# Moving a recurrence's last stage and the latent preparations into the operators' stage

## The reference, cut to what matters

```
rwkv7 (6 heads):  state = state * w_t - (state . kk_t) b_t + v_t k_t ;  y_t = state . r_t
gated delta (6):  A = tril(k k^T * decay * beta, -1);  u, w = solve(I + A, [v*beta, k*beta*exp(gc)])
                  per chunk: delta = u - w S;  o = q S + attn delta;  S = d S + k^T delta
latent attention: q = rms(c_q) w_uq;  kv = rms(c_kv) w_ukv;  ang = positions * inv_freq
                  rope with cos(ang), sin(ang) on 32 of 96 columns; softmax; times v
out:              gates silu(gate), group norms, w_out, then the feed-forward layer
```

## Time and profile before

| | us |
|---|---|
| median of 3 runs | 2176.77 |
| fastest run | 2175.23 |
| profiled execution, its own time | 2175.9 |
| its span | 2174.1 |

### The profile page before, as it was taken

One profiled execution on the slowest core, in us unless ns is written; L12 is line 12 of the kernel. 1 busy time (PEld: TensorE's weight loads), 2 busy tenths in 40 slices (PEclk: granted clock), 3 DMA queues, 4 the chain that ended last, 5 costly groups with the idle time before them and its releaser, 6 DMA issues. The chain is left out here.

```text
span 2174.1 us, 35768 instructions
## 1 busy us (share of the span) xinstructions
PE 2119.3 (97%) x14084; PEld 1693.3 (78%) x14084; DVE 1294.8 (60%) x1761; ACT 908.6 (42%) x1422; POOL 119.5 (5%) x96
## 2 busy tenths in 40 slices
PE   9999999999999999999999999999887899999999
PEld 6888788888877777778888887777777467888887
DVE  7565676663379877576665349596465566433333
ACT  5444532222366666652222236555332545323221
POOL 0000011110000000001111000000243000000000
PEclk9999999999999999999999999999999899999999
DMA  7331333333324221323333332222000112333331
GB/s 270 101 133 39 88 116 96 96 96 97 96 73 150 80 71 48 106 71 109 97 96 102 97 97 78 85 84 81 3 4 4 47 39 70 114 96 98 97 96 67
DMA packets 54231, 189.77 MB, mean 87 GB/s; under 512 B 5984, under 2 KB 6240, under 8 KB 53984
## 3 DMA queue, kind: packets, MB, share of 16 engines
q1 hardware_dynamic: 53824, 187.49, 28.1%
q10 hardware_dynamic: 288, 0.59, 0.1%
HBM read 184.91 MB, written 3.15 MB: 86 GB/s over the span
## 5 line engine op out<-in xcount | busy, mean ns | idle before, releaser
L303 PE MATMUL l_banks<-l_r_hi,l_w_hi 128*128 128x512 f32 x1440 | 573.5, 398 | 2.5 <-DVE l_r_lo L1544 2.3
L305 PE MATMUL l_banks<-l_r_hi,l_w_lo 128*128 128x512 f32 x1440 | 561.0, 390 | 0.0
L304 PE MATMUL l_banks<-l_r_lo,l_w_hi 128*128 128x512 f32 x1440 | 560.8, 389 | 0.0
L282 ACT ACTIVATE l_w_hi<-ring 128x1024 fp32r<-128x1024 f32 x217 | 228.4, 1056 | 280.6 <-PE l_banks L305 278.0
L288 DVE TENSOR_TENSOR l_w_lo<-ring,l_w_hi 128x1024 fp32r<-128x1024 f32 x217 | 299.8, 1384 | 73.4 <-ACT l_w_hi L282 69.8
L303 PEld LDWEIGHTS l_banks<-l_r_hi,l_w_hi 128*128 128x128 f32 x1440 | 270.3, 188 | 71.2 <-issue 8.2
L304 PEld LDWEIGHTS l_banks<-l_r_lo,l_w_hi 128*128 128x128 f32 x1440 | 270.5, 188 | 57.1 <-issue 3.8
L305 PEld LDWEIGHTS l_banks<-l_r_hi,l_w_lo 128*128 128x128 f32 x1440 | 270.3, 188 | 57.3
L303 PE MATMUL mt_a<-net_r_hi,net_w_hi 128*128 128x512 f32 x352 | 137.3, 390 | 0.0
L305 PE MATMUL mt_a<-net_r_hi,net_w_lo 128*128 128x512 f32 x352 | 137.0, 389 | 0.0
L304 PE MATMUL mt_a<-net_r_lo,net_w_hi 128*128 128x512 f32 x352 | 136.9, 389 | 0.0
(11 more groups left out here) (566 smaller groups left out, 3542.7 us busy)
## 6 DMA issues: line engine op xcount, KB each, us to landing
ring<-weights SPq DMA_DIRECT2D x314, 512.0 KB, 3.6
na_bias<-window_bias SPq DMA_DIRECT2D x16, 512.0 KB, 5.5
da_rel<-t_rel SPq DMA_DIRECT2D x8, 448.0 KB, 4.6
outT<-X SPq DMA_DIRECT2D x12, 256.0 KB, 2.1
X<-xT SPq DMA_DIRECT2D x8, 256.0 KB, 5.2
const<-consts SPq DMA_DIRECT2D x1, 1312.0 KB, 10.4
l_pt<-pT SPq DMA_DIRECT2D x2, 512.0 KB, 9.7
X<-outT SPq DMA_DIRECT2D x4, 256.0 KB, 3.2
```

The costliest lines, as they stand in the source:

```text
L282: act.activation(self.w_hi[:, c % self.slots, :], k.ring[:, g % RING, :], ACT.Copy).then_inc(self.w_rounded, 1)
L303: pe.matmul(psum, hi, self.hi(rhs_slot), start=start, stop=False)
L304: pe.matmul(psum, hi, self.lo(rhs_slot), start=False, stop=False)
L305: return pe.matmul(psum, lo, self.hi(rhs_slot), start=False, stop=stop)
```

## The change

1. The stage `recurrence` is gone. Its carries and outputs of pair 5 (`carry_last`, `outputs_last`) stand at the end of the operators' stage. Its preparations stand within pair 5: the four transfers on SP after earlier conditions, ScalarE's work in pieces after levels 2, 3 and 4 of pair 5, VectorE's angles before `carry_out(1)` and their reduction after `carry_out(6)`, TensorE's sums after `finish_yn`.
2. A second buffer M, `m2`: masks alternate, and a mask waits for the level before the last one.
3. `chunk_ends(1)` and `(2)` move from behind `mask(i, 0)` to behind `mask(i, 2)`.
4. `setup_akr(0)` stands before `turn_u(0)`, `invert_x(0, 0)` rather than behind them.
5. States of the recurrence live in other tiles, and the eight banks of PSUM (`hy_ps`) are held over both stages.

```diff
@@ -2168,22 +2168,23 @@
         v_tok = st.sb("v_tok", [P, 2, TT, P])
         b_tok = st.sb("b_tok", [P, TT, P])
         ki_tok = st.sb("ki_tok", [P, TT, P])
-        more = st.sb("more", [P, 2, W])
+        m2 = st.sb("m2", [P, U8, CHUNK])
...
-        ps = st.ps("ps", [P, 8, S])
         P_B = 2
         SETUP = (3, 4, 7)
         F0, F1 = 5, 6
...
-        homes = [unused[:, j * W:(j + 1) * W] for j in range(3)] + [more[:, 0, :], more[:, 1, :], b_tok[:, :, :].rearrange("p t s -> p (t s)")[:, 0:W]]
+        unused = [akr[:, 0, :, :, :].rearrange("p u k l -> p (u k l)"), kx[:, 0, :, :].rearrange("p u l -> p (u l)")]
+        homes = [unused[j // 3][:, j % 3 * W:(j % 3 + 1) * W] for j in range(5)] + [b_tok[:, :, :].rearrange("p t s -> p (t s)")[:, 0:W]]
         def state(c):
@@ -2191,6 +2192,16 @@
                 return n0[:, 0:EARLY, 0, :]
             return homes[c - 2].rearrange("p (n d) -> p n d", d=CHUNK)
+        squares = [k.H[:, j, :] for j in (0, 2, 4)]
+        last_homes = ki_tok[:, :, :].rearrange("p t s -> p (t s)").rearrange("p (c d) -> p c d", d=CHUNK)
+        r32 = slice(0, MLA_ROPE)
+
+        def last_state(c):
+            return n0[:, PAIRS - 1, 0, :] if c == 1 else last_homes[:, c - 2, :]
+
+        def last_bank(c):
+            return F1 if c % 2 else SETUP[2]
+
         def y_bank(c):
             return S_B if c == NCH - 1 else SETUP[1 + (c + 1) % 2]
@@ -2256,6 +2267,17 @@
             return slice(t * P + c * CHUNK, t * P + c * CHUNK + CHUNK)
         with k.nc.Block() as block:
+            @block.sync
+            def _(sp):
+                sp.wait_ge(s["q_out"], MIX_T + 1)
+                sp.dma_start(la.pos, bass.AP(k.dram["positions"].tensor, 0, [[0, P], [1, S]])).then_inc(s["pos_loaded"], 16)
+                sp.wait_ge(s["a_ps"], PAIRS)
+                sp.wait_ge(s["ar_ps"], PAIRS)
+                sp.dma_start(la.mc, k.dram["mla_consts"]).then_inc(s["mc_loaded"], 16)
+                sp.dma_start(la.uq, k.dram["w_uq"]).then_inc(s["up_loaded"], 16)
+                sp.dma_start(la.ukv, k.dram["w_ukv"]).then_inc(s["up_loaded"], 16)
+                sp.wait_ge(s["up_loaded"], 32)
+
             @block.tensor
             def _(pe):
@@ -2443,7 +2465,7 @@
                         for pair in DIAG:
                             for c, h in pair:
                                 u = TT * h + t
-                                mm = pe.matmul(xt_ps(h, t)[half(c ^ h)], M[half(c), u, :], U[i % 2][half(c), u, :], start=True, stop=True)
+                                mm = pe.matmul(xt_ps(h, t)[half(c ^ h)], M[n % 2][half(c), u, :], U[i % 2][half(c), u, :], start=True, stop=True)
                     mm.then_inc(s["xt_ps"], 1)
@@ -2501,18 +2523,34 @@
                                            keys(n)[half(h), c * CHUNK:(c + 1) * CHUNK], start=True, stop=True)
                     mm.then_inc(s["y_ps"], 1)
+                def carry_last(c):
+                    if c >= 2:
+                        pe.wait_ge(s["carried"], NCH - 2 + c - 1)
+                    for h in range(2):
+                        mm = pe.matmul(ps[half(h), F0, 0:CHUNK], mt[half(h), last, c, :], last_state(c)[half(h), :], start=True, stop=True)
+                    mm.then_inc(s["carry_ps"], 1)
+
+                def outputs_last(c):
+                    if c == NCH - 1:
+                        pe.wait_ge(s["carried"], NCH - 2 + c - 1)
+                    pe.wait_ge(s["y_added"], 2 * (NCH - 1) + max(c - 2, 0))
+                    for h in range(2):
+                        mm = pe.matmul(ps[half(h), last_bank(c), 0:CHUNK], last_state(c)[half(h), :],
+                                       keys(last)[half(h), c * CHUNK:(c + 1) * CHUNK], start=True, stop=True)
+                    mm.then_inc(s["y_ps"], 1)
+
                 last = PAIRS - 1
                 setup_a(0)
                 setup_ar(0)
                 setup_tokens(0)
                 for i in range(PAIRS):
                     nxt = i + 1 < PAIRS
+                    if i == 0:
+                        setup_akr(0)
                     turn_u(i)
                     invert_x(i, 0)
                     if i:
                         finish_wu(i - 1)
-                    else:
-                        setup_akr(0)
                     invert_p(i, 0)
                     if i:
@@ -2563,6 +2601,22 @@
                 outputs(6)
                 outputs(7)
                 finish_yn(last)
+                pe.wait_ge(s["lat_squared"], 3)
+                pe.wait_ge(s["u_out"], LV * PAIRS)
+                pe.matmul(la.ms[:, 0, :], k.c("ones"), squares[0], start=True, stop=False)
+                pe.matmul(la.ms[:, 0, :], k.c("ones"), squares[1], start=False, stop=True).then_inc(s["lat_summed"], 1)
+                pe.wait_ge(s["yn_out"], 2 * PAIRS)
+                pe.wait_ge(s["mt_out"], PAIRS)
+                carry_last(1)
+                for c in range(1, NCH):
+                    outputs_last(c)
+                    if c == 1:
+                        pe.matmul(la.ms[:, 1, :], k.c("ones"), squares[2], start=True, stop=True).then_inc(s["lat_summed"], 1)
+                    elif 2 <= c < 2 + TT:
+                        at = (c - 2) * P
+                        pe.matmul(la.ms[:, 2, c - 2:c - 1], squares[2][:, at:at + P], k.c("ones")[:, 0:1], start=True, stop=True).then_inc(s["lat_summed"], 1)
+                    if c + 1 < NCH - 1:
+                        carry_last(c + 1)
             @block.scalar
@@ -2643,14 +2697,38 @@
                     if nxt:
                         tokens(i + 1)
                     xt_out(i, 2)
+                    if not nxt:
+                        act.wait_ge(s["masked"], LV * EARLY)
+                        act.wait_ge(s["wu_ps"], EARLY)
+                        for j in range(3):
+                            act.activation(squares[j], la.cg[j], ACT.Square).then_inc(s["lat_squared"], 1)
                     xt_out(i, 3)
+                    if not nxt:
+                        act.wait_ge(s["lat_squared"], 3)
+                        for j in range(3):
+                            act.activation(la.cg[j], la.cg[j], ACT.Copy, scale=k.p("q_norm", j) if j < 2 else k.p("kv_norm")).then_inc(s["lat_scaled"], 1)
+                        act.wait_ge(s["mc_loaded"], 16)
+                        act.wait_ge(s["gq_done"], 1)
+                        act.activation(la.c("rot4"), la.c("rot4"), ACT.Copy, scale=la.gq[:, 1:2]).then_inc(s["lat_scaled"], 1)
+                        act.activation(la.c("rot_rep", r32), la.c("rot_rep", r32), ACT.Copy, scale=k.p("k_qk", 1, r32)).then_inc(s["lat_scaled"], 1)
                     xt_out(i, 4)
+                    if not nxt:
+                        for j in range(MIX_T):
+                            act.activation(pi[:, G_GATE + j, :], pi[:, G_GATE + j, :], ACT.Silu).then_inc(s["silued"], 1)
                     if nxt and not delta(i + 1):
                         x1(i + 1)
                     if not delta(i):
                         keys_out(i)
                 wu_out(PAIRS - 1)
+                act.wait_ge(s["trig"], 1)
+                act.activation(la.sn, la.r, ACT.Sin).then_inc(s["sin_done"], 1)
+                act.activation(la.cs, la.r, ACT.Sin, scale=0.5).then_inc(s["sin_done"], 1)
+                act.preload_act_table_set(LN_EXP)
                 yn_out(PAIRS - 1)
+                act.wait_ge(s["silued"], MIX_T)
+                act.wait_ge(s["lat_scaled"], 5)
+                act.wait_ge(s["sin_done"], 2)
+                act.wait_ge(s["lat_summed"], 2 + TT)
             @block.gpsimd
@@ -2678,11 +2756,11 @@
                 def mask(i, lv):
                     n = LV * i + lv
-                    if n:
-                        pool.wait_ge(s["xt_ps"], n)
+                    if n >= 2:
+                        pool.wait_ge(s["xt_ps"], n - 1)
                     if lv == 0:
                         pool.wait_ge(s["a_out"], 2 * i + 2)
-                    pool.tensor_tensor(M, A[i % 2], over(level(lv + 1)), ALU.mult).then_inc(s["masked"], 1)
+                    pool.tensor_tensor(M[n % 2], A[i % 2], over(level(lv + 1)), ALU.mult).then_inc(s["masked"], 1)
                 mask(0, 0)
                 chunk_ends(0)
@@ -2691,6 +2769,8 @@
                     nxt = i + 1 < PAIRS
                     mask(i, 1)
                     mask(i, 2)
+                    if 0 < i < MIX_T:
+                        chunk_ends(i)
                     if nxt and delta(i + 1):
                         decay_masks(i + 1)
                     mask(i, 3)
@@ -2699,8 +2779,6 @@
                         diagonal(i)
                     if nxt:
                         mask(i + 1, 0)
-                        if not delta(i + 1):
-                            chunk_ends(i + 1)
             @block.vector
@@ -2841,6 +2919,30 @@
                         dve.tensor_tensor(out, out, ps[:, y_bank(c), at:at + to * CHUNK].rearrange("p (n d) -> p n d", d=CHUNK),
```

(44 more changed lines are left out.)

119 lines of the change are left out of this document (8 added, 111 removed).

## The result

The changed kernel takes 2164.76 us (median of five, 2158.93 to 2166.09), against 2176.77 of the kernel before beside it (three runs, 2175.23 to 2177.77): ratio 0.9946, interval 0.9935 to 0.9957, or 11.8 us less. A second set, on a chip where the kernel before took 2174.19, gave 0.9952 (0.9938 to 0.9965), 10.4 us less by the ratio and 9.5 by the two medians. Two further runs of the kernel before, of 3394.2 and 3028.5 us, are left out of all comparisons. The forecast was 2167.5 us, 8.85 less than the profiled execution before. The range held and the class (within 2%) was right; by the ratios the forecast gain was 1.5 to 3 us too small.

The account below looks back on a forecast made before the run. TensorE, busy 97% of the span, sets most of the time; the recurrence stage is a chain no engine fills. -7.25 - 1.5 - 0.7 + 0.6 = -8.85 from 2175.9 gives 2167.05, 2167.9 against the median; said 2167.5, range 2162 to 2173.

Parts of the forecast that it names:

- The end of the recurrence, -7.25: From pair 5's n0 to the mixer's end: 1.1 for sums, 6.0 carries and outputs, 1.0 stage change; 8.1 replaces 15.35 us.
- The rival with the sums at the low clock: Sums over partitions ahead of the carries at low clock: 2.55 us less gain, 2170; 25%, alone or with angles held.
- The first pair, -1.5: Pair 0: key products in TensorE's idle time and a mask wait of 0.79 gone save about 1.5 us (0.7 to 2.0).
- The scalings, -0.7: Preparation of pair 1: moved scalings no longer hold L2795 (1.53 to 0.68 us); 0.7 us less, nothing taken for pair 2.
- The angles, +0.6: Pair 5, VectorE's angles ahead of carry_out(1), partly held by POOL's masks: 0.6 us lost on the path, between 0 and 2.3.
- Its upper end of 2.3: Angles in pair 5 held by POOL's mask and `diagonal`: 2.3 us lost rather than 0.6, giving 2169.
- ScalarE's pieces and the reduction: Pair 5 preparations on ScalarE, and VectorE's reduction of 2.5 us before add_outputs(4): nothing lost, at most 0.5 us each.
- The slow rival: TensorE's instruction blocks late beside the transfers: one delay 2171, three 2178.5; one or two 4%, three or more 3%.
- that one wrong sign (over 1 us): TensorE rows with "issue" of over 1 us behind the transfers would show the prediction wrong.
- a better clock in the mixer's end: At the mixer's end's start ScalarE and VectorE split weights whatever TensorE's clock; a better clock gives a microsecond at most.

Follow-up runs that it names:

- one_buffer: The changed kernel with one masked-A buffer in place of two, each mask waiting for the product before it; 2164.43 us, ratio 0.9953 to the kernel before.
- transfers_ahead: The kernel before with only the recurrence stage's four transfers issued in the operators' stage, where the changed kernel issues them; 2171.37 us, ratio 0.9989 to the kernel before.
- merge_alone: The changed kernel with second buffer, early key products and moved scalings undone; the recurrence stays merged into the operators' stage; 2166.55 us, ratio 0.9962 to the kernel before.
- after_again: The changed kernel run once more, unchanged, on another chip; 2164.73 us, ratio 0.9952 to the kernel before.
- warm_end: The changed kernel plus six TensorE products without use behind outputs_last(2) to outputs_last(7); 2163.95 us, ratio 0.9949 to the kernel before.
- keys_behind: The changed kernel with pair 0's key products behind invert_x(0, 0) again; 2166.68 us, ratio 0.9964 to the kernel before.
- spread_warm: The changed kernel with the third sum cut into four products behind outputs_last(2) to (5), plus two products without use; 2162.41 us, ratio 0.9947 to the kernel before.

## Why the prediction came out as it did

- **The end of the recurrence, -7.25.** Right in mechanism and nearly in size: -7.83, the same to 0.01 in every merged kernel that leaves the end alone. Within it the sums came out at 0.76 behind n0 rather than 1.10, the carries and outputs at 5.39 behind the sums rather than 6.0, the stage change at 1.37 rather than 1.00. In the 5.39 the period was 0.69 rather than 0.65, and the third sum added 0.75 rather than 1.13. The rival with the sums at the low clock did not occur.
- **The first pair, -1.5.** The step that was mis-sized. It measured 2.5 at pair 0's second copy and 2.0 by pair 3. Each part went the way that was said, and further: from the stage's start, update 0 begins 2.0 us earlier (10.02 to 8.00) for 1.2 forecast, and level 1's `invert_x` 2.7 (12.19 to 9.51) for 1.5. The sum took the key products as they were, 1.78 us for 27, and did not ask why: they ran at the low clock, after the very pause into which the change moves them. The whole 32 take 1.10 at the full clock. Also its credit was wrong: the mask wait goes by the order of the products, and the second buffer does nothing (one_buffer).
- **The scalings, -0.7.** Failed. The row became short in after as said and TensorE's wait of 0.72 went, but the row was long by where POOL's instructions fell in one execution: with the scalings where they were it is 1.77 (beside a mask, transfers_ahead) and 0.69 (merge_alone), with them moved 0.68 (after) and 1.77 (after_again). The step took one trace's meeting of two instructions for a property of the order.
- **The angles, +0.6.** The lock was judged rightly by the two-input rows and the skill's rule: the Trainium skill (SBUF — State Buffer, section "Who interferes with whom") lets `tensor_scalar` contend, and the rows of 1.40 and 1.15 against 0.43 agree. Its upper end of 2.3 did not follow, since VectorE was idle there and TensorE's gap of 0.87 "issue" is at 1678.83 still. The path lost 0.1 in the mean of nine traces, and 0.6 to 0.7 in the two of the changed kernel.
- **The rest.** ScalarE's pieces and the reduction cost nothing that a distance shows. The slow rival did not occur: behind the transfers the longest row with "issue" is 0.98 us in after, as in before, and 1.26 in after_again, so that one wrong sign (over 1 us) did show there. The prediction also gave a better clock in the mixer's end a microsecond at most; in warm_end's one trace it was worth 2.7.

What the traces give as systematic is then 7.8 at the end and 3.2 by pair 3 (mean of the old order 81.1 in the three traces without the other edits, of the new 77.9), less 0.1: 10.9, beside 10.4 and 11.8 measured. The profiles differ by more, since before's execution had two low stretches and after's had none. Of the 3.2, 2.0 is the key products by keys_behind; the other 1.2 rests on that one trace, and neither the buffer nor the scalings alone show it: this stays open. What sets off the chance stretches, the two later ones and that in the first 5 us, stays open too.

## What to carry to other kernels

A duration from a low-clock stretch is not a property of the instruction: look what TensorE did just before, and if the edit fills that pause, take the row's full-clock price on both sides. Compare two single traces by distances between fixed points, and have a second trace of the same kernel before a difference of 1 or 2 us is given to an edit. Look behind a chain of tiny products as well: twelve of the thirteen traces have a low clock in the next stage's first 5 us. And before a better clock, or a short row, is put down to an edit, look whether a trace without the edit has it too.

## What the runs showed of the hardware

- TensorE's clock fell in the operators' stage by execution: none or two stretches in the same program (after, after_again), none, one or two over all kernels, each at a cost of 1.3 to 2.1 us. A further one, in the stage's first 5 us (0.66 to 0.71), came in six of thirteen traces.
- After a chain of tiny products and a pause of 1.4 to 2 us at the stage change, the next stage's first 5 us ran at 0.50 to 0.67 in twelve of thirteen traces. With filler of 0.47 us per period they ran at 1.00 in one trace (warm_end) and at 0.66 in another, with needed sums in four of the gaps (spread_warm).
- `tensor_scalar` fp32 128x512 on VectorE: 0.43 alone, 1.38 to 1.40 when it starts behind a GpSimd instruction, in each of the nine traces in which the angles stand ahead of `carry_out(1)`; in five of them the next one took 1.15 beside POOL's next instruction.
